# The second block's rows of per-feature factors through DRAM, in place of diagonals and matmuls

## The reference

```python
x = rms_norm(x, final_norm)                        # end of the first block
# second block, in each layer
sh_m, sc_m, gt_m, sh_f, sc_f, gt_f = ada_chunks(c, w_ada[layer], b_ada[layer])
...
h = h + gt_m * rms_norm_2(y, g_post_m)             # y: the mixer's output
f = conv_ffn(modulate(h, g_pre_f, sh_f, sc_f), ...)
h = h + gt_f * rms_norm_2(f, g_post_f)
# the same for the context stream in layer 0, with factors of its own
```

## Time and profile before

| | |
|---|---|
| median of three runs | 1957.99 us |
| span of the profiled execution, first to last instruction | 1956.7 us |
| PE (TensorE matmul) busy | 1913.7 us, 98% |
| PEld (weight load, beside PE) busy | 1629.3 us, 83% |
| DVE (VectorE) busy | 1273.9 us, 65% |
| ACT (ScalarE) busy | 922.8 us, 47% |
| POOL (GpSimd) busy | 14.1 us, 1% |
| moved by DMA | 320.62 MB, 164 GB/s |

### The profile page before, as it was taken

The page is one execution under the profiler, slowest core; times in us unless marked ns, Lnnn a source line. Parts: engine busy times, 40 slices in busy tenths (PEclk is TensorE's granted clock), DMA queues, the critical chain, the costliest instruction groups (busy, mean ns, idle before and its releaser), DMA issues.

```text
span 1956.7 us, 28779 instructions
## 1 busy us (share of the span) xinstructions
PE 1913.7 (98%) x11994; PEld 1629.3 (83%) x11994; DVE 1273.9 (65%) x1670; ACT 922.8 (47%) x1300; POOL 14.1 (1%) x17
## 2 busy tenths in 40 slices
PE   7999999999999999999999999999999999989998
PEld 6888969888888888788879878988888889679997
DVE  5776796766676668776664464765554367757774
ACT  5334565334533455643454355543333345755553
POOL 0000000000000000000000110000000000000000
PEclk9999999999999999999999999999999999999999
DMA  7876536765476642776453211222323223024552
GB/s 279 283 274 218 186 105 224 280 257 216 157 277 253 229 174 95 272 274 252 152 174 107 108 44 65 101 94 86 108 86 108 87 86 109 23 86 165 180 194 87
DMA packets 46065, 320.62 MB, mean 164 GB/s; under 512 B 5233, under 2 KB 5361, under 8 KB 7921
## 3 DMA queue, kind: packets, MB, share of 16 engines
q1 hardware_dynamic: 39024, 270.09, 38.4%
q10 hardware_dynamic: 6912, 48.69, 6.5%
HBM read 317.72 MB, written 1.05 MB: 163 GB/s over the span
## 4 chain that ended last, share of the span: by engine, by line
PE 92%; DVE 4%; ACT 2%; issue 1%; DMA 0%; DVEq 0%; ACTq 0%
PE ps L532 89%; PE ps L873 1%; DVE s_big L2181 1%; DVE s_wl L1890 1%; PE ps L734 0%; ACT s_wh L1228 0%; PE ps L711 0%; DVE s_st L2120 0%; ACT s_big L1398 0%; DVE s_tmp L2410 0%; DVE ps L2114 0%; DVE s_X L2386 0%; PE ps L835 0%; DVE s_X L2076 0%; DMA s_X<-in_x 0%
## 5 line engine op out<-in xcount | busy, mean ns | idle before, releaser
L532 PE MATMUL ps<-s_xx,s_wh 128*128 128x512 f32 (+1 forms) x3328 | 899.6, 348 | 11.2 <-DVE s_wl L1960 10.0
L1890 DVE TENSOR_TENSOR s_wl<-s_raw,s_wh 128x2048 fp32r<-128x2048 f32 x213 | 487.4, 2290 | 293.5 <-ACT s_wh L1228 293.4
L532 PE MATMUL ps<-s_xx,s_wl 128*128 128x256 f32 (+1 forms) x2208 | 670.2, 304 | 0.4 <-DVE s_xx L2413 0.4
L532 PEld LDWEIGHTS ps<-s_xx,s_wh 128*128 128x128 f32 x3328 | 579.7, 190 | 106.4 <-DVE s_wl L1960 10.3
L1228 ACT ACTIVATE s_wh<-s_raw 128x2048 fp32r<-128x2048 f32 x213 | 404.7, 1907 | 133.0 <-PE ps L532 129.7
L532 PEld LDWEIGHTS ps<-s_xx,s_wl 128*128 128x128 f32 x2208 | 419.4, 190 | 19.6 <-issue 3.2
L532 PE MATMUL ps<-s_wh,s_hl 128*128 128x512 f32 (+1 forms) x608 | 232.3, 382 | 0.5 <-DVE s_hl L1982 0.5
L532 PE MATMUL ps<-s_wh,s_hh 128*128 128x512 f32 (+1 forms) x608 | 230.0, 378 | 0.0
L532 PE MATMUL ps<-s_wl,s_hh 128*128 128x512 f32 (+1 forms) x608 | 229.8, 378 | 0.0
L532 PE MATMUL ps<-s_wh,s_xx 128*128 128x256 f32 x928 | 179.4, 287 | 0.0
L1342 ACT ACTIVATE s_tmp<-s_tmp 128x512 f32<-128x512 f32 x44 | 27.8, 632 | 281.2 <-DVE s_tmp L2007 274.5
(11 more groups left out here) (235 smaller groups left out, 1680.9 us busy)
## 6 DMA issues: line engine op xcount, KB each, us to landing
s_big<-in_w_ada ACTq DMA_DIRECT2D x46, 1024.0 KB, 6.1
s_raw<-in_ffn_down SPq DMA_DIRECT2D x44, 1024.0 KB, 4.8
s_raw<-in_w_up SPq DMA_DIRECT2D x44, 1024.0 KB, 4.8
s_raw<-in_ffn_gate SPq DMA_DIRECT2D x43, 1024.0 KB, 5.1
s_raw<-in_ffn_up SPq DMA_DIRECT2D x43, 1024.0 KB, 4.8
s_raw<-in_w_down SPq DMA_DIRECT2D x22, 1024.0 KB, 4.8
s_raw<-in_w_in SPq DMA_DIRECT2D x18, 1024.0 KB, 4.8
s_raw<-in_w_in_ab SPq DMA_DIRECT2D x10, 1024.0 KB, 4.8
```

The source lines that it names most:

```text
L532: return pe.matmul(o, lhsT, rhs, start=start, stop=stop, skip_group_check=True)
L1890: dve.tensor_tensor(wide(wl, u), raw[:, u % SLOTS, :].rearrange("p (k n) -> p k n", k=8), f32(wide(wh, u)), SUB).then_inc(*w_low.tick(u))
```

## The change

The six rows are written to a DRAM tensor `gain_dram` [6, 1024] as columns: each write takes 128 partitions x 8 elements to DRAM, so that neighbouring elements in DRAM come from neighbouring partitions and every element is a piece of its own. They are read back in halves, 512 elements repeated for 128 partitions. ACT issues all of it. `final_norm` is written in the first feed-forward (block 2). The other five rows are written one after the other at block 7 of the last down projection of the first block; the two halves of "final" are read at block 8 behind them. ("m",0,0) and ("f",0,1) are read at unit 2 of layer 0's attention, ("m",0,1) at unit 8, ("f",0,0) after block 3 of the up projection, and ("m",1,0) at unit 2 of layer 1's attention. The diagonals, matmuls and evictions go, and with them their turns in the bank rotation of layer 0's up projection, whose order is changed too. DVE waits for the reads where it waited for the evictions. The diff is cut to its core:

```diff
 
...
+        final_out, gains_out = signal("final_out", 16), signal("gains_out", 16)
+        gain_in = {key: signal("gain_in_" + "".join(map(str, key)), 16) for key in
+                   ("final", ("m", 0, 0), ("m", 0, 1), ("f", 0, 0), ("f", 0, 1), ("m", 1, 0))}
...
-        def gain_columns(key, h):
-            if key == "final":
-                return v("final_norm", 4 * h, 4)
-            c = 8 * {"m": 2, "f": 5}[key[0]] + 4 * h
-            return mod[:, key[1], c:c + 4, key[2]]
+        gain_at = {"final": 0, ("m", 0, 0): 1, ("m", 0, 1): 2, ("f", 0, 0): 3, ("f", 0, 1): 4, ("m", 1, 0): 5}
+
+        def gain_halves(key):
+            rows = gain_rows[key]
+            return [(rows[h], gain_dram[gain_at[key]:gain_at[key] + 1, 512 * h:512 * h + 512].to_broadcast([128, 512]))
+                    for h in range(2)]
...
-        conv_banks = [[0, 3, 4, 7, 1, 5, 6, 2], [2, 3, 4, 5, 6, 7, 0, 1]]
+        conv_banks = [[0, 3, 4, 7, 1, 2, 5, 6], [2, 3, 4, 5, 6, 7, 0, 1]]
...
-
-            def gains(key, banks):
-
-                for h, b in enumerate(banks):
-                    claim(b)
-                    pe.wait_ge(*gain_diag[key, h])
-                    mm(ps[b][:, :], const("mean256"), gain_diags[key][h], True, True).then_inc(
-                        *product.tick(("gain", key, h)))
-                    freed[b] = gain_row[key, h]
...
                     if n == 2:
-                        gains(("m", 0, 0), (4, 5))
                         value(1)
                     attend(H, n)
-                gains(("m", 0, 1), (6, 7))
...
-                    if j in aside:
-                        gains(aside[j], banks())
                 conv_down(s, l, streams, down_aside)
...
-            def gains(key, banks):
-
-                for h, b in enumerate(banks):
-                    act.wait_ge(*product["gain", key, h])
-                    act.activation(gain_rows[key][h], ps[b][:, :], ACT.Copy, scale=256.0).then_inc(
-                        *gain_row.tick((key, h)))
+            def final_written():
+                act.wait_ge(*vec_in[0])
+                act.dma_start(gain_dram[0:1, :].rearrange("o (k p) -> p (o k)", p=128), v("final_norm", 0, 8),
+                              allow_slow_non_contiguous=True).then_inc(
+                    *final_out.tick(0))
+
+            def gains_written():
+
+                act.wait_ge(*modulated[0])
+                act.wait_ge(*modulated[1])
+                for key in (("m", 0, 0), ("m", 0, 1), ("f", 0, 0), ("f", 0, 1), ("m", 1, 0)):
+                    c, at = {"m": 16, "f": 40}[key[0]], gain_at[key]
+                    act.dma_start(gain_dram[at:at + 1, :].rearrange("o (k p) -> p (o k)", p=128),
+                                  mod[:, key[1], c:c + 8, key[2]], allow_slow_non_contiguous=True).then_inc(*gains_out.tick(0))
+
+            def gains(key, free):
+
+                act.wait_ge(*free)
+                act.wait_ge(*(final_out if key == "final" else gains_out)[0])
+                for rows, written in gain_halves(key):
+                    act.dma_start(rows, written).then_inc(*gain_in[key].tick(0))
...
                     if n == 2:
-                        gains(("m", 0, 0), (4, 5))
+                        gains(("m", 0, 0), mixed["even", "u", 3])
+                        gains(("f", 0, 1), mixed["even", "u", 3])
                         value(1)
+                    if n == 8:
+                        gains(("m", 0, 1), masked["even", 5, 1])
...
-                gains(("m", 0, 1), (6, 7))
...
                     if j in aside:
-                        gains(aside[j], [rotation[(r[0] + c) % 8] for c in range(ns)])
-                        r[0] += ns
+                        gains(aside[j], y_out[("m", 0, 1), 3])
...
-                gains(("m", 1, 0), (0, 1))
+                gains(("m", 1, 0), y_out[("f", 0, 0), 3])
...
-            ffn("ffn1", 0, {4: lambda: sines(1), 7: lambda: sines(0)})
+            ffn("ffn1", 0, {2: final_written, 4: lambda: sines(1), 7: lambda: sines(0)})
...
-                    8: lambda: (ctx_tokens(0), ctx_tokens(1)),
-                    10: lambda: (ctx_tokens(2), ctx_tokens(3), gains("final", (5, 6)))})
+                    7: gains_written, 8: lambda: (gains("final", x_low[("pre", 0, 1), 3]), ctx_tokens(0), ctx_tokens(1)),
+                    10: lambda: (ctx_tokens(2), ctx_tokens(3))})
...
-            def gain_diagonals(key, *halves):
-                for h in halves:
-                    dve.tensor_tensor(gain_diags[key][h].rearrange("p (k n) -> p k n", n=128),
-                                      const("ident").unsqueeze(1).to_broadcast([128, 4, 128]),
-                                      gain_columns(key, h).unsqueeze(2).to_broadcast([128, 4, 128]), MUL).then_inc(
-                                          *gain_diag.tick((key, h)))
...
-                dve.wait_ge(*gain_row[B, 1])
+                dve.wait_ge(*gain_in[B][0])
...
-                    dve.wait_ge(*gain_row["final", b // 2])
+                    dve.wait_ge(*gain_in["final"][0])
...
-                gain_diagonals(("m", 0, 0), 0, 1)
                 for n in range(len(H.units) + 3):
-                    if n == 9:
-                        dve.wait_ge(*masked["even", 7, 1])
-                        gain_diagonals(("m", 0, 1), 0, 1)
...
-                    if j + 1 in aside:
-                        gain_diagonals(aside[j + 1], 0, 1)
-                    if j in aside:
-                        r[0] += ns
...
-                gain_diagonals(("m", 1, 0), 0, 1)
...
-            def final_gains():
-                dve.wait_ge(*x_low[C, 3])
-                gain_diagonals("final", 0, 1)
```

## The result

The changed kernel takes 1968.66 us (median, 1965.99 to 1969.11) and the kernel before, on the same chip, 1958.12 us: a ratio of 1.0047, 95% interval 1.0035 to 1.0059. It is slower by 0.5%, where 0.5% faster was expected. The profiled execution has a span of 1966.8 us, 10.1 more than before.

A forecast was written before the change was run, and what follows sets the result against it. PE, busy 98% of the span, was taken to bound the kernel. Removing six matmul pairs saves 10.0 us of the 1956.7 us span, giving 1946.7, plus 1.3 to the median: 1948.0 us; range 1945.8 to 1954.5.

The forecast's parts named there:

- The pairs: Six pairs of fp32 matmuls with mean256 removed from PE, each priced 0.95 to 1.97 us; sum 10.04 us gained.
- Rival E: Set up for the follow-ups: the pairs were never worth anything, so removing them saves nothing on the path; no chance given.
- rival 4: The pairs' time is not regained because what is removed was hidden: 1957 to 1958 us; chance 0.02.
- DVE's diagonals in the attention: Two diagonals of ("m",0,1) removed from DVE, set against two row-load issues on ACT: 0, bounds -0.6 and +0.7 us.
- The issue time: Five column writes in ACT's queue near 1009 us: 0.334 to 0.6 us each, costing nothing up to 0.63 us.
- rival 1: Column writes hold ACT over 0.63 us each; at 2.7 us a 10.2 us stall, 1958.2 us; chance 0.15.
- The transfers: Column writes ahead of the final rows on ACT's DMA queue: 11 to 25 ns a packet, 4 to 8 us, hidden.
- 28 ns: Price per packet, 325 packets per DMA engine, above which the final rows land too late and PE stalls.
- third rival: Small writes are dear, final rows land late: gain used up at 59 ns a packet, 1964.3 us at 78; chance 0.10.
- my limit of 1033.7: Time in us after which landing of the final rows would stall PE, 24.5 us after the first write's issue.

The follow-up runs named there:

- the kernels with spread pieces: Kernel before plus five unread column writes at block 7, pieces 64 or 512 bytes apart in DRAM: 1959.63 us (1.0003) and 1959.05 us (1.0007).
- The second group: DVE's residual updates in the changed kernel with columns turned once on PE and stored as rows (1949.18, again 1947.53 us); the first group is the kernel before.
- The third group: DVE's residual updates in the changed kernel, with five column writes in a bunch at block 7: 1968.66 us.
- the good one: Changed kernel without column writes: columns gathered by DVE, turned once on PE, stored as 48 rows: 1949.18 us, ratio 0.9945; again 1947.53 us, 0.9943.
- the kernel with the writes alone: Kernel before plus the five column writes at block 7, which nothing reads: 1975.73 us against 1958.45, ratio 1.0082.
- the run that is 2.6 us late: Kernel before plus three waited-for writes of 1024 words, pieces 4, 16 and 64 bytes apart, in the odd mixer's attention: 1961.39 us.

## Why the prediction was wrong

**The pairs: right.** The second group less the first gives -1.75, -5.51, -8.97 and -10.24 us. So "final" brought 1.75 (1.82 expected, and the one transposition is in it), ("m",0,0) and ("m",0,1) together 3.76 (3.79), ("f",0,0) and ("f",0,1) together 3.46 (3.48), and ("m",1,0) 1.27 (0.95; it was the one with ACT late next). The sum is 10.24 where 10.04 stood. A pair's price read from the step that it puts into the rhythm of its neighbours held within 0.1 us for the first three of these differences; the last one was 0.3 us too low. Rival E and my rival 4 fall with it. DVE's diagonals in the attention, taken at 0 with bounds of -0.6 and +0.7, have no row of their own, but the 3.76 leaves them next to nothing.

**Where the gain went.** The third group less the second: 18.94, 20.41, 20.44 and 20.39 us. The changed kernel is the good one plus a single stall of 19.4 us, and 1.0 us that stood ahead of it. DVE's last row ahead of the column writes, which stands at 1005.11 us in the good kernel, in the changed one:

```profile
1006.11 0.68 DVE L2316 TENSOR_TENSOR s_xx<-s_tmp,s_xx 128x512 fp32r<-128x512 f32 x1
```

That 1.0 us isn't the change's: it came with the granted clock of this one execution (last section). By 1043 us the stall has brought 17.9 us, nearly all of it PE's three waits, and 1.5 more come behind it, 1.2 of them from the matmuls at half clock; from there on the two kernels run alike. 20.4 lost, 10.2 won: +10.1 us of span.

**The issue time: mis-sized, and no cause.** I took 0.33 to 0.6 us for each write and named 0.63 as the limit. The first two took 0.38 and 0.61, the next three 3.33 together, 0.86 in the mean over all. By my rival 1 that would have cost 5 x (0.86 - 0.33) - 1.5 = 1.2 us. The kernels with spread pieces have the same issue time and cost 0.6 to 1.4 us at the ratio, within their intervals of nothing. What I had not thought of is the 6.56 us for two row loads: ordinary DMAs, issued in 0.84 us where no column write stands ahead of them. That they were held because the writes hadn't drained is argued and not shown. It is the 3.4 us of PE's first two waits.

**The transfers: the step that failed.** It failed three times. The price: "a 4-byte packet is nearer to the 72-byte one; I take 11 to 25 ns". The 72-byte packets were loads, and the choice was between a load and a store of 2 KB, neither of which says anything of neighbouring small writes. Over 1000 to 1060 us, q10 with its 5488 packets (5200 of the writes, 288 of the row loads) had 34.9% of the engines, 335 us, or 61 ns each. That is over the 28 ns at which I had PE stall, and just over the 59 ns at which my third rival had the gain used up; that it meets the loss so well is luck, as the next paragraph shows. The range's upper end, 1954.5, left this rival out; the bounds of the unknown cost, 11 and 78 ns, had it in. I gave it 0.10 although the row on its side, the only store of the trace, was as near by kind (a write to DRAM) as the load was by size.

The measure: I took what a transfer costs as its packets times their time on an engine, so that 28 ns a packet was the limit. Three writes have 21 ns a packet, inside the 11 to 25 that I took, and lose 10 us; five in the kernel with the writes alone have 38 ns, well under 59, and lose 16; one has 9 ns and takes 12.4 us to land, and its packets are a microsecond of that. What counted was the time to landing, of the writes and of what was in flight beside them, and my sum had no term for it but the 2.2 us of the output.

The victim: I counted the weight loads of the other queue as a fixed 11.9 us of the engines' time and let only the final rows come late. In the trace it was the reverse in order: the weight tile that landed at 1039.1 held ACT, DVE and PE, while the rows, whose two halves were issued at 1012.1 and 1018.3 and landed 29.1 and 27.3 us later, at 1041.2 and 1045.6, were there when DVE used them at 1047.5. They were 12 us over my limit of 1033.7 and cost nothing, since PE stood still already. Here the writes delayed everything that was in flight, and what was needed first was on the critical path.

**The rule that spoke against it.** The Trainium skill (DMA: Bandwidth & Descriptors, Rules for kernel authors) has one descriptor for each element of a strided last dimension. The trace agrees: 1040 packets a write (16 of them the semaphore's), and the reads had them too, for 9 ns each. The Trainium skill's same page, Specifications, has a read-modify-write below 512 bytes. By the size of the pieces alone, those 16, 64 or 512 bytes apart would have been as dear as those side by side; they landed in 3.5 and 3.1 us alone and in 4.3 to 7.7 us in bursts, and cost nothing, and the 32-byte pieces landed in 1.4 us. So the size below 512 bytes by itself isn't what decided here; whether a read-modify-write of a shared stretch has a part in the slow case, no run shows. The measurements decide: the slow case is that of 4-byte pieces with another piece right beside them. A sentence of the Trainium skill on another case, DMA between cores, in the same page's section Back-pressure in remote DMA, describes the victim better than my sum did: stalled writes stall the other queues of the engine that makes them. The trace agrees, with 2.7 us for a weight packet on q1 in place of 0.33, while q10's packets took 223 ns.

**What stays open.** The runs show at which spacing it happens (at 4 bytes, not at 16), not what in the memory or on the way to it does it; 8 bytes wasn't tried, and 16 bytes only as one write where DMA was idle, by its landing time. Why five writes cost between 13 and 22 us from run to run isn't shown either. The range from one (nothing) to three (10 us) was not filled in.

## What to carry to other kernels

Write a vector that lies across partitions to DRAM only after turning it on PE, as rows: here one transposition was enough, and the one store of 48 rows landed in 1.5 us, where 1024 4-byte pieces side by side took 12 us as a single write and up to 38 in a burst. Before adding DMAs of a form that the trace doesn't show, ask what other transfers are in flight at that place and how late each may be, not only who reads the new data; don't take the packets' time on the engines for the time to landing; and if a bound of the unknown price reaches past break-even, keep that case in the range. If such writes can't be avoided, issue them one at a time where loads have slack: the same five writes cost some 20 us in a bunch (1968.66 against 1949.49 us) and nothing that shows on the whole when spread out.

## What the hardware showed unexpectedly

- 1024 writes of 4 bytes, side by side in DRAM, land after 12.4 us beside weight loads. Where DMA is idle, they land after 9.1 us in runs of eight from one partition and after 3.5 us 16 bytes apart; read rather than written they take 2.4 us, and as 128 pieces of 32 bytes 1.4 us.
- They pass the engines at 7 to 9 ns a packet at first; in a burst of five writes the later packets show 61 and 223 ns, so the packets' time at the start of a burst doesn't tell what it costs.
- Meanwhile a 1 MB load on another queue lands in 13.2 us in the median in place of 4.8, and the issue of two ordinary loads on the same queue as the writes takes 6.56 us in place of 0.84.
- The profiled executions differ by up to 2.6 us at the first mixer, 302 us in, ahead of every edit but the lone first write, and keep most of it. The granted clock goes with it: over 284 to 300 us it is 0.89 in the kernel before and in the one that turns the columns, 0.68 in the changed one, which is 2.0 us late behind it, and 0.79 in the run that is 2.6 us late (1.1 of that from before it). Over 786 to 800 us it is 0.76 in the kernel before and 0.88 in the changed one, which gets 0.9 us back. With landmarks like those above this can be told from an effect of the change.
